# Hybrid decoder step: attention probabilities split to f16 halves by token and turned by DMA instead of TensorE

## The chip, the cores and the metric

The kernel runs on one core of a Trainium2 chip. The metric is the device time of one execution in microseconds (us), and each kernel is quoted with the median of its runs.

## What is computed

Two layers of one mixer each. 2048 prompt tokens (16 tiles of 128) and 32 sample tokens (8 sequences of 4) pass through both.

```python
h = rms_norm(x, norm_g); p = einsum('ntd,de->nte', h, w_in)
qa, ka, va, ga, qb, kb, vb, gb = split(p)
qa = rotary(rms_norm(qa, q_norm_g)); ka = rotary(rms_norm(ka, k_norm_g))
s = where(mask, qa . ka * 64**-0.5, -inf)      # window of 128 tokens, 8 heads on 2 key heads
m = maximum(max(s), sink); e = exp(s - m)
attn = (e / (sum(e) + exp(sink - m))) . va
ret = retention(qb, kb, vb)                    # chunks of 128 tokens, 4 heads
x = x + concat(silu(ga) * attn, silu(gb) * rms_norm(ret)) @ w_out
```

## The kernel before

A layer has four stages, named after the weights in use: A (attention and its gate), B0 and B1 (two retention heads each) and O (the output projection). A stage goes through 17 steps, in A first the sample (step 0), then the 16 prompt tiles. Every engine has its own program written out by hand, and semaphores tie them together.

Numbers of float32 range are carried as two f16 halves, high and low, and a product takes three matmuls. ScalarE writes the high half, VectorE the low one (`scalar_tensor_tensor`: scale, then subtract the high half).

In stage A, while TensorE projects tile s (`proj`, three pieces with 24 matmuls each, in the banks PA and PB by turns), the attention of the tiles before it is put between the pieces:

- `a_T` (L551, L553) transposes q and k of tile s-1 on TensorE. ScalarE's `a_tout` writes their high halves, VectorE's `a_lo` (L943, L945) the low halves.
- `a_S` computes the scores of head group g (0 or 1) in the banks S0 and S1. VectorE's `a_softmax` adds the mask and takes the maximum (L1003), then finds the negative maximum and the sink's share (L1009, L1011). ScalarE's `a_exp` (L1564) makes the probabilities `prob`.
- `a_PT` (L598) turns them by eight f32 transposes on TensorE into X0 and X1. ScalarE's `a_pout` (L1577) and VectorE's `a_plo` (L979) make f16 halves of them, key-wise.
- `a_PV` multiplies by the values into OB. VectorE's `a_mix` has the reciprocal of the sum (L1020 to L1023) and multiplies by the gate (L1043).

VectorE also has, in each step, `a_land_q` (L892, L896), `a_land_k` (L908, L912), a reciprocal square root of 12 small dependent operations (L914, L811 to L817), `a_rotate` (L923 to L937), `a_vcopy` (values to f16, L967 and L968) and `gate` (L957). In eight steps it has `w_low` twice (L851, the next stage's weights), in four others `w_absmax` (L834).

In a helper `Chain`, every small dependent operation is followed at once by a wait for its end. `a_tanh` (L1530) on ScalarE ends a step: it waits for the third piece of the projection, and `gate` waits for it.

In layer 0 the prompt's hidden states are made during stage A: `p_squares` and `p_high` (ScalarE), `p_rstd` and `p_low` (VectorE), `p_T` (L1923, a DMA transpose issued by SyncE). SyncE has one queue, in which these, the loads and the stores of `mix` stand in order. ScalarE's `a_kv` of step 2 waits for the stores of the sample's keys and values (`kvs_out`), which stand behind `p_T(7)` in that queue.

## Time and profile before

| | us |
|---|---|
| median of 3 runs (lowest, highest) | 2010.08 (2008.51, 2020.27) |
| the profiled execution's time | 2014.24 |
| its span, first to last instruction | 2012.4 |
| TensorE busy in the span | 1858.1 (92%) |
| VectorE busy | 1442.5 (72%) |
| ScalarE busy | 712.0 (35%) |

The mean granted TensorE clock is 0.978. Stage A of layer 0 takes roughly 50 to 410 us of the span, that of layer 1 1070 to 1405 us. Busy shares are means over stages whose limits differ: a wait or an engine has to be read inside a stage.

### The profile page before, as it was taken

To read this page: it belongs to the slowest core of one execution; us is meant where nothing else is said; L and a number is where in the kernel's file an instruction comes from. 1 tells how busy PE (TensorE), PEld (TensorE's weight loads), DVE (VectorE), ACT (ScalarE), POOL (GpSimd) and SP (SyncE) were. 2 spreads that over 40 slices of the span, in tenths; PEclk is the share of its full clock that TensorE was granted. 3 is DMA by queue.
4 is the path that set the end of the run, shared out by engine and by line. 5 is a ranking of instruction groups with operands and counts; after the bars stand their busy time and mean duration, and the time that the engine had idled before them with its cause. 6 is when DMAs were issued, how large, how long until landed. Compare 5 with 4: busy or idle time off the path is not lost.

```text
span 2012.4 us, 36841 instructions
## 1 busy us (share of the span) xinstructions
PE 1858.1 (92%) x12264; PEld 1047.5 (52%) x12264; DVE 1442.5 (72%) x4918; ACT 712.0 (35%) x1841; POOL 68.5 (3%) x108
## 2 busy tenths in 40 slices
PE   1778999997999999978998999999999999999999
PEld 0445555553555555543444655555555555555444
DVE  6679899976665666677885899999666657666542
ACT  4444565541232213232442455555213221232110
POOL 3010000010000000021001000001000000000000
PEclk9899999998999999999999999999999999999999
DMA  8332222032000210079994000001210021003864
GB/s 245 67 120 53 58 52 53 16 130 83 11 11 10 98 61 11 11 152 264 242 244 135 8 16 16 10 16 57 78 51 10 10 97 62 11 10 92 225 202 143
DMA packets 203403, 163.03 MB, mean 81 GB/s; under 512 B 145073, under 2 KB 175985, under 8 KB 203153
## 3 DMA queue, kind: packets, MB, share of 16 engines
q1 hardware_dynamic: 193584, 126.33, 23.2%
q0 software_dynamic: 9728, 35.66, 5.4%
q8 instruction: 38, 0.62, 0.1%
q14 instruction: 53, 0.43, 0.1%
HBM read 88.75 MB, written 41.16 MB: 65 GB/s over the span
## 4 chain that ended last, share of the span: by engine, by line
PE 60%; DVE 21%; ACT 4%; issue 4%; DMA 2%; SPq 1%; DVEq 0%; ACTq 0%
PE PA L499 24%; PE PB L499 24%; DVE r L1003 3%; ACT r L1564 2%; DVE r L979 2%; DVE mix L1043 2%; PE S L646 2%; PE OB L665 2%; PE TK L635 1%; PE S L681 1%; PE OB L672 1%; PE X L598 1%; DVE w_mx L834 1%; DMA r<-r 1%; DMA out<-land 1%
## 5 line engine op out<-in xcount | busy, mean ns | idle before, releaser
L499 PE MATMUL PA<-w_a,hT 128*128 128x512 f16 (+1 forms) x1920 | 405.2, 362 | 13.2 <-DVE land L957 13.2
L499 PE MATMUL PB<-w_a,hT 128*128 128x512 f16 (+1 forms) x1920 | 405.2, 362 | 0.0
L499 PEld LDWEIGHTS PA<-w_a,hT 128*128 (+1 forms) x1920 | 186.2, 99 | 187.5 <-DVE land L957 14.1
L499 PEld LDWEIGHTS PB<-w_a,hT 128*128 (+1 forms) x1920 | 185.8, 99 | 180.5 <-issue 11.8
L499 PE MATMUL PA<-w_b,hT 128*128 128x512 f16 x768 | 182.5, 389 | 16.8 <-DVE land L957 16.8
L499 PE MATMUL PA<-w_b,r 128*128 128x512 f16 x768 | 174.4, 384 | 19.4 <-DMA r<-r 17.1
L1564 ACT ACTIVATE r<-r,nm,unqk 128x256 f32<-128x256 f32 x256 | 150.5, 589 | 109.9 <-DVE sd L1011 109.9
L499 PE MATMUL PB<-w_b,hT 128*128 128x512 f16 x768 | 176.3, 379 | 0.0
L1622 ACT ACTIVATE r<-OB 128x128 f32<-128x128 f32 (+1 forms) x136 | 36.3, 272 | 389.8 <-PE S L681 362.4
L499 PE MATMUL PB<-w_b,r 128*128 128x512 f16 x768 | 171.3, 379 | 0.0
L1092 DVE TENSOR_TENSOR r<-S,t_dec 128x256 f32<-128x256 f32 x64 | 27.2, 425 | 154.4 <-PE S L646 154.2
L499 PEld LDWEIGHTS PA<-w_b,r 128*128 128x128 f16 x768 | 75.1, 99 | 114.2 <-DMA r<-r 18.1
L499 PEld LDWEIGHTS PA<-w_b,hT 128*128 (+1 forms) x768 | 76.0, 100 | 106.3 <-DVE land L957 17.2
L499 PEld LDWEIGHTS PB<-w_b,r 128*128 128x128 f16 x768 | 75.0, 98 | 90.1 <-DVE r L1194 0.9
L499 PEld LDWEIGHTS PB<-w_b,hT 128*128 (+1 forms) x768 | 74.8, 98 | 77.2 <-issue 0.4
L1003 DVE CUSTOM_DVE_ANT_0 r<-S,t_ma 128x256 f32<-128x256 f32 x256 | 93.1, 420 | 12.6 <-PE S L586 6.9
L1634 ACT ACTIVATE r<-r,minv 128x1024 f16<-128x1024 f32 (+1 forms) x34 | 39.1, 1149 | 143.0 <-DVE minv L1155 136.4
L1577 ACT ACTIVATE r<-X 128x512 f16<-128x512 f32 x128 | 69.3, 594 | 51.4 <-PE X L598 51.4
L979 DVE SCALAR_TENSOR_TENSOR r<-X,r 128x512 f16<-128x512 f32 x128 | 82.0, 682 | 4.6 <-ACT r L1577 4.6
L586 PE MATMUL S<-kT_hi,r 64*128 64x256 f16 x512 | 54.3, 276 | 27.3 <-DVE r L945 27.3
L598 PE MATMUL X<-eye,r 128*128 128x128 f32 x544 | 71.7, 275 | 7.7 <-ACT es L1567 7.7
L1123 DVE SCALAR_TENSOR_TENSOR r<-r,S 128x128 f32<-128x128 f32 x120 | 29.1, 284 | 60.9 <-PE S L681 60.7
(247 smaller groups left out, 2784.0 us busy)
## 6 DMA issues: line engine op xcount, KB each, us to landing
out<-r SPq DMA_DIRECT2D x40, 512.0 KB, 4.7
r<-mixed SPq DMA_DIRECT2D x32, 512.0 KB, 4.1
r<-in_x_prompt SPq DMA_DIRECT2D x25, 512.0 KB, 4.3
w_b<-in_w_in POOLq DMA_DIRECT2D x16, 512.0 KB, 9.0
mixed<-mix SPq DMA_DIRECT2D x32, 256.0 KB, 2.0
w_a<-in_w_in POOLq DMA_DIRECT2D x16, 512.0 KB, 8.6
mixed<-mix SPq DMA_DIRECT2D x64, 128.0 KB, 1.8
w_b<-in_w_out POOLq DMA_DIRECT2D x16, 512.0 KB, 7.5
```

Of the source, the lines that this page charges most:

```text
L499: last = nc.tensor.matmul(out[0:s.rows, 0:n], lhs, w16(ph, k, p, wpart), start=(k == 0 and part == 0 and wpart == 0), stop=(k == KT - 1 an ...
L586: last = nc.tensor.matmul(SS[kv][:, i * 256:(i + 1) * 256], qT16[d, q, h * P:(h + 1) * P], kT[d, :, :].rearrange("p b t -> p (b t)"), star ...
L598: last = nc.tensor.transpose(XX[q // 4][:, (q % 4) * P:(q % 4 + 1) * P], prob[:, q * P:(q + 1) * P], eye[:, :])
L646: last = nc.tensor.matmul(S0[0:r, h * r:(h + 1) * r], qkT[:, (2 + h) * r:(3 + h) * r], qkT[:, h * r:(h + 1) * r], start=True, stop=True)
L665: nc.tensor.matmul(OB[0:r, h * P:(h + 1) * P], stm[0:r, h * r:(h + 1) * r], v, start=True, stop=s.first)
L979: last = V.scalar_tensor_tensor(out=pT16[:, 1, c], in0=XX[q][:, :], scalar=P_TOP, in1=pT16[:, 0, c], op0=ALU.mult, op1=ALU.subtract)
L1003: last = V.tensor_tensor_reduce(out=prob[:, h * 256:(h + 1) * 256], in0=SS[h // 2][:, (h % 2) * 256:(h % 2) * 256 + 256], in1=m, scale=1.0 ...
L1043: last = V.scalar_tensor_tensor(out=mix[:, b, m:m + A_DIM], in0=OB[:, o:o + A_DIM], scalar=rr[:, g, h:h + 1], in1=land[:, b, A_W + 2 * KV_ ...
L1564: A.activation(x, x, ACT.Exp, scale=unqk[:, 0:1], bias=nm[:, g, h:h + 1], accum_out=rsum[:, g, h:h + 1])
L1577: last = A.activation(pT16[:, 0, c], XX[q][:, :], ACT.Copy, scale=P_TOP)
L1622: last = A.activation(osq[0:r, h * P:(h + 1) * P], OB[0:r, h * P:(h + 1) * P], ACT.Square, accum_out=oss[0:r, h:h + 1])
L1634: A.activation(mh_of(s)[0:r, 0, :], mxt[0:r, b, :], ACT.Copy, scale=minv[0:r, b:b + 1]).then_inc(o_hi, 1)
```

## The change

- The probabilities stay token-wise. ScalarE (`a_phi`) and VectorE (`a_plo`) make the f16 halves from `prob_t` in SBUF, and SyncE issues one DMA transpose for each head group (`prob_T`). `a_PT` and `a_pout` remain for the sample alone. `a_softmax` of a tile waits until the halves of the tile before it, same group, are turned (`a_tp`).
- Scores of group 0 go to S0 and S1, those of group 1 to X0 and X1; `a_PV` of group 1 writes the bank TK. Both scores are issued together, and `a_PV` and `a_mix` of tile s-2 stand in step s.
- VectorE's order in a step is new: `gate` of the tile before comes first, `a_mix` of tile s-2, group 1, last. Waits in chains of small operations are put off, with other work between (`put`, `wait`, `a_norm_link`, `a_rr_link`). The high half of the values moves to ScalarE (`a_vhigh`); `a_rotate` has two wide multiplications in place of four.
- `a_tanh` waits for `a_mix` of tile s-2, both groups, and so does `a_T`.
- In layer 0 the low halves of tiles 4 to 16 move from VectorE to GpSimd (`late_low`, two operations each). The x of tiles 8 to 16 is loaded at the start, in rows of 64 elements, into `hT`. `p_rstd` runs for four groups, not seven. The sinks are loaded before tiles 2 and 3, and the layer's small gain operations (`layer_gains`) stand ahead of the layer.

```diff
 
 RING = 6
...
+CVA = 8
 CVO = 8
 
...
-                        pe.wait_ge(a_po, 2 * an(L, s))
+                        pe.wait_ge(a_po, 2 * L + 2)
                     pe.wait_ge(a_qk, an(L, s) + 1)
                     if not s.first:
-                        pe.wait_ge(a_sm, 2 * an(L, s))
+                        pe.wait_ge(a_sm, 2 * an(L, s) - 1)
+                    if not (s.fixed and s.c < 3):
+                        pe.wait_ge(a_mx, 2 * an(L, s) - 2)
...
+                else:
+                    pe.wait_ge(a_sm, 2 * n)
...
-                                last = nc.tensor.matmul(SS[kv][:, i * 256:(i + 1) * 256],
+                                last = nc.tensor.matmul((SS, XX)[g][kv][:, i * 256:(i + 1) * 256],
...
+                else:
+                    pe.wait_ge(a_tp[g], 16 * tn(L, s) + 16)
+                    if g == 0:
+                        pe.wait_ge(a_vl, tn(L, s) + 1)
+                    pe.wait_ge(a_mx, 2 * n if s.first else 2 * n + g - 1)
...
-            def a_work(L, s, old=True):
-
-
-                late = old and not (s - 2).sample
+            def a_work(L, s):
+
+                t, u = s - 1, s - 2
 
                 def f0():
-                    if old:
-                        a_PV(L, s - 2, 0)
-                    if old and not late:
-                        a_PT(L, s - 2, 1)
-                    if not (s - 1).sample:
-                        a_T(L, s - 1)
-                    if late:
-                        a_PT(L, s - 2, 1)
+                    if not t.sample and u.sample:
+                        a_PV(L, u, 0)
+                        a_PT(L, u, 1)
+                    if not t.sample:
+                        a_T(L, t)
 
                 def f1():
-                    if (s - 1).sample:
-                        a_T(L, s - 1)
+                    if t.sample:
+                        a_T(L, t)
                     else:
-                        a_S(L, s - 1, 0)
+                        a_S(L, t, 0)
+                        a_S(L, t, 1)
 
                 def f2():
-                    if old:
-                        a_PV(L, s - 2, 1)
-                    if (s - 1).sample:
-                        a_S(L, s - 1, 0)
+                    if t.sample:
+                        a_S(L, t, 0)
                         cached_keys(1).then_inc(s_ct, 1)
+                    else:
+                        a_PV(L, u, 1 if u.sample else 0)
 
                 def f3():
-                    a_PT(L, s - 1, 0)
-                    a_S(L, s - 1, 1)
+                    if t.sample:
+                        a_PT(L, t, 0)
+                        a_S(L, t, 1)
+                    elif not u.sample:
+                        a_PV(L, u, 1)
 
                 return [f0, f1, f2, f3]
 
...
+            def a_vlow(L, s):
+
+                v.wait_ge(a_vh, tn(L, s) + 1)
+                V.scalar_tensor_tensor(out=v16[:, s.par, 1, :], in0=land[:, s.par, A_W + KV_W:A_W + 2 * KV_W],
+                                       scalar=cs["A"][:, 2:3], in1=v16[:, s.par, 0, :],
+                                       op0=ALU.mult, op1=ALU.subtract).then_inc(a_vl, 1)
...
-                if s.sample:
-                    return
-                v.wait_ge(a_po, 2 * an(L, s) + g + 1)
-                for q in range(2):
-                    c = slice(q * 512, (q + 1) * 512)
-                    last = V.scalar_tensor_tensor(out=pT16[:, 1, c], in0=XX[q][:, :], scalar=P_TOP,
-                                                  in1=pT16[:, 0, c], op0=ALU.mult, op1=ALU.subtract)
-                last.then_inc(a_pl, 1)
+                v.wait_ge(a_ph, 2 * tn(L, s) + g + 1)
+                V.scalar_tensor_tensor(out=ph16[g][:, 1, :], in0=prob_t[g], scalar=P_TOP, in1=ph16[g][:, 0, :],
+                                       op0=ALU.mult, op1=ALU.subtract).then_inc(a_pl, 1)
...
                 alone(v, a_s, n + 1)
+                if not s.sample and not (s.fixed and L == 0 and s.first):
+                    alone(v, a_tp[g], 16 * tn(L, s))
...
-            for q in range(4):
+            w_absmax(0, "A", 0)
+            w_absmax(0, "A", 1)
+            p_rstd(0)
+            for q in range(2, KT):
                 w_absmax(0, "A", q)
-            p_rstd(0)
+            w_top(0, "A")
             p_low(0)
-            w_absmax(0, "A", 4)
-            w_absmax(0, "A", 5)
-            p_low(1)
-            w_absmax(0, "A", 6)
-            w_absmax(0, "A", 7)
-            w_top(0, "A")
-            p_low(2)
             w_scale(0, "A")
             for q in range(KT):
                 for c in range(3):
                     w_low(0, "A", q, c)
-            p_low(3)
-            v.wait_ge(c_ld, CONST_LOADS * 16)
+                if q in (1, 3, 5):
+                    p_low((q + 1) // 2)
+            v.wait_ge(sk_ld, SINK_LOADS * 16)
+            layer_gains(0)
...
+                def a_first(s):
+
+                    if s.sample:
+                        a_land_q(L, s)
+                        ch = a_land_k(L, s)
+                        gate("A", L, s, 2, A_W, A_W + 2 * KV_W)
+                        a_norm(s, ch)
+                        if L == 0:
+                            v.wait_ge(c_ld, CONST_LOADS * 16)
+                        a_rotate(L, s, ch)
+                        return
+                    a_land_q(L, s)
+                    a_softmax(L, s - 1, 0)
+                    V.memset(v16[:, 0, :, :], 0.0)
+                    ch = a_land_k(L, s)
+                    a_norm(s, ch)
+                    a_rotate(L, s, ch)
+                    a_softmax(L, s - 1, 1)
...
                 def a_step(s, k=None):
-                    if not (s.fixed and s.c < 2):
-                        a_lo(L, s - 1)
-                    a_land_q(L, s)
-                    if not (s.fixed and s.c < 2):
-                        a_plo(L, s - 2, 1)
-                    if not s.sample:
-                        a_softmax(L, s - 1, 0)
-                    if not (s.fixed and s.c < 2):
-                        a_mix(L, s - 2, 1)
-                    if not s.sample:
-                        a_vcopy(L, s - 1)
-                    if k is not None:
-                        w_low(L, "B0", k, 0)
+
+                    t, u = s - 1, s - 2
+                    gate("A", L, t, 2, A_W, A_W + 2 * KV_W)
+                    if u.sample:
+                        a_mix(L, u, 0)
+                        a_lo(L, t)
+                        a_land_q(L, s)
+                        old = a_rr(L, u, 1)
+                        for i in range(3):
+                            a_rr_link(u, 1, old, i)
+                    else:
+                        a_plo(L, u, 1)
+                        m0 = a_rr(L, u, 0)
+                        a_rr_link(u, 0, m0, 0)
+                        a_vlow(L, u)
+                        a_rr_link(u, 0, m0, 1)
+                        a_lo(L, t)
+                        a_rr_link(u, 0, m0, 2)
+                        m1 = a_rr(L, u, 1)
+                        a_rr_link(u, 1, m1, 0)
+                        a_land_q(L, s)
+                        a_rr_link(u, 1, m1, 1)
+                    a_softmax(L, t, 0)
+                    if not u.sample:
+                        a_rr_link(u, 1, m1, 2)
+                    a_softmax(L, t, 1)
                     ch = a_land_k(L, s)
-                    if not s.sample:
-                        a_softmax(L, s - 1, 1)
-                    if not s.sample:
-                        a_plo(L, s - 1, 0)
-                    a_rotate(L, s, ch)
-                    gate("A", L, s, 2, A_W, A_W + 2 * KV_W)
-                    if not s.sample:
-                        a_mix(L, s - 1, 0)
-                    if k is not None:
-                        w_low(L, "B0", k, 1)
-
...
+                    if not u.sample:
+                        a_norm_link(s, ch, 0)
+                        a_mix(L, u, 0, m0)
+                        a_norm_link(s, ch, 1)
+                        if k is not None:
+                            w_low(L, "B0", k, 0)
+                        a_norm_link(s, ch, 2)
+                        if k is not None:
+                            w_low(L, "B0", k, 1)
+                        a_norm_link(s, ch, 3)
+                        a_norm_link(s, ch, 4)
+                        a_norm_link(s, ch, 5)
+                        a_norm_link(s, ch, 6)
...
+                        a_norm_link(s, ch, 11)
+                        a_rotate(L, s, ch)
+                        a_plo(L, t, 0)
+                        a_mix(L, u, 1, m1)
+                    else:
+                        a_norm(s, ch)
+                        a_rotate(L, s, ch)
+                        a_mix(L, u, 1, old)
+                        a_plo(L, t, 0)
...
                 r = s.rows
                 act.wait_ge(pe_piece, piece("A", L, s, 2) + 1)
+                if not (s.fixed and s.c < 2):
+                    act.wait_ge(a_mx, 2 * an(L, s) - 2)
...
+            def a_phi(L, s, g):
+
+                act.wait_ge(a_ex, 2 * an(L, s) + g + 1)
+                A.activation(ph16[g][:, 0, :], prob_t[g], ACT.Copy, scale=P_TOP).then_inc(a_ph, 1)
+
+            def a_vhigh(L, s):
+
+                act.wait_ge(a_pv, 2 * an(L, s))
+                A.activation(v16[:, s.par, 0, :], land[:, s.par, A_W + KV_W:A_W + 2 * KV_W], ACT.Copy,
+                             scale=cs["A"][:, 2:3]).then_inc(a_vh, 1)
...
                 def a_step(s, k=None):
-                    tail, old = not s.sample, not (s.fixed and s.c < 2)
-                    late = old and not (s - 2).sample
-                    if old and not late:
-                        a_pout(L, s - 2, 1)
-                    if tail and not (s - 1).sample:
-                        a_tout(L, s - 1)
-                    if late:
-                        a_pout(L, s - 2, 1)
+
+                    t, u = s - 1, s - 2
+                    if u.sample:
+                        a_pout(L, u, 1)
+                    else:
+                        a_phi(L, u, 1)
+                        a_vhigh(L, u)
+                    a_tout(L, t)
                     a_q(L, s)
-                    if tail and (s - 1).sample:
-                        a_tout(L, s - 1)
                     if k is not None:
                         w_high(L, "B0", k, 0)
                     a_kv(L, s)
-                    if tail:
-                        a_exp(L, s - 1, 0)
-                        if (s - 1).sample:
-                            act.wait_ge(s_ct, L + 1)
-                            cached_keys_out().then_inc(s_ce, 1)
-                        a_pout(L, s - 1, 0)
+                    a_exp(L, t, 0)
+                    a_phi(L, t, 0)
                     if k is not None:
                         w_high(L, "B0", k, 1)
-                    if tail:
-                        a_exp(L, s - 1, 1)
+                    a_exp(L, t, 1)
                     a_tanh(L, s)
 
...
                         p_high(7)
-                    if c in (3, 5, 7, 9, 11):
-                        p_squares(c + 5)
-                        if c < 11:
-                            p_squares(c + 6)
-                    if c in (4, 6, 8, 10, 12):
+                        p_squares(8)
+                        p_squares(9)
+                    if c == 2:
+                        p_squares(10)
+                        p_squares(11)
+                    if c == 3:
+                        p_squares(12)
+                        p_squares(13)
+                    if c == 4:
+                        p_squares(14)
+                        p_squares(15)
+                        p_squares(16)
+                    if 4 <= c <= 12:
                         p_high(c + 4)
...
+            def late_low(n):
+
+                alone(pool, x_hi, n + 1)
+                G.tensor_scalar(x_of(n), x_of(n), py[:, n:n + 1], None, ALU.mult).then_inc(ch_late, 1)
+                alone(pool, ch_late, n - 3)
+                G.tensor_tensor(xh_of(n, 1), x_of(n), xh_of(n, 0), ALU.subtract).then_inc(x_lo, 1)
...
+            def prob_T(L, s, g):
+
+                alone(sp, a_pl, 2 * tn(L, s) + g + 1)
+                alone(sp, a_pv, 2 * an(L, s) if s.first else 2 * an(L, s) + g - 1)
+                sp.dma_start_transpose(pT16[g].rearrange("p e (c t) -> p (e c) t", t=P),
+                                       ph16[g].rearrange("p e n -> p (e n)")).then_inc(a_tp[g], 16)
...
-                for n in range(3, PRO):
+                p_T(3)
+                for n in range(PRO, STEPS):
+                    load_px(n)
+                for n in range(4, PRO):
                     p_T(n)
...
+                def a_step(s):
+                    if not (s.fixed and s.c < 3):
+                        prob_T(L, s - 2, 1)
+                    prob_T(L, s - 1, 0)
+                    if not (s.fixed and s.c < 3):
+                        store_mix("A", L, s - 2)
...
+                    for c in range(2, STEPS):
+                        if 5 <= c <= 13:
+                            p_T(c + 3)
+                        a_step(Step(c))
```

## Rows read from the trace of the kernel before

**Rows 1.** Stretches of both stages A: us; busy PE, PEld, DVE, ACT, POOL; clock; DMA; GB/s
```profile
1190.00:1380.00 190.00, 182.47 (x1611) 112.97 (x1612) 175.49 (x685) 106.94 (x291) 0.35 (x1) 1.00 0.04 14
150.00:395.00 245.00, 220.46 (x1886) 137.50 (x1887) 226.13 (x864) 137.85 (x358) 0.34 (x1) 0.97 0.19 47
```

**Rows 2.** waits in layer 1's attention steps: us in total, times, longest
```profile
DVE r L1003 <- DVE rs L817: 3.4, 14, 0.3
...
DVE r L1003 <- PE S L586: 0.6, 2, 0.4
```

**Rows 3.** timeline of VectorE, one step of layer 1: start us, us
```profile
1345.95 0.75 DVE L892 SCALAR_TENSOR_TENSOR land<-PA,cs_A,qk_g 128x512 f32<-128x512 f32 x1
...
1347.20 1.28 DVE L979 SCALAR_TENSOR_TENSOR r<-X,r 128x512 f16<-128x512 f32 x2
...
1350.23 0.16 DVE L1020 TENSOR_TENSOR rr<-rsum,es 128x4 f32<-128x4 f32 x1
...
1350.90 0.86 DVE L1043 SCALAR_TENSOR_TENSOR mix<-OB,rr,land 128x64 f32<-128x64 f32 x4
1351.67 0.28 DVE L967 TENSOR_SCALAR r<-land,cs_A 128x128 f16<-128x128 f32 x1
1351.98 0.35 DVE L968 SCALAR_TENSOR_TENSOR r<-land,cs_A,r 128x128 f16<-128x128 f32 x1
1352.40 0.75 DVE L851 SCALAR_TENSOR_TENSOR w_b<-w_b,w_gs  x1
1353.07 0.34 DVE L908 SCALAR_TENSOR_TENSOR land<-PB,cs_A,qk_g 128x128 f32<-128x128 f32 x1
...
1353.64 0.17 DVE L914 TENSOR_SCALAR ss<-ss 128x10 f32<-128x10 f32 x1
...
1356.41 0.42 DVE L1003 CUSTOM_DVE_ANT_0 r<-S,t_ma 128x256 f32<-128x256 f32 x1 [0.27 <-DVE rs L817]
...
1365.37 0.75 DVE L892 SCALAR_TENSOR_TENSOR land<-PB,cs_A,qk_g 128x512 f32<-128x512 f32 x1
...
1383.99 0.75 DVE L892 SCALAR_TENSOR_TENSOR land<-PA,cs_A,qk_g 128x512 f32<-128x512 f32 x1 [0.69 <-ACT r L1507]
```

**Rows 4.** timeline of TensorE, the turning of the probabilities in layer 1
```profile
1391.18 1.04 PE L598 MATMUL X<-eye,r 128*128 128x128 f32 x8
```

**Rows 5.** VectorE's L892, once a step: first to last start in a window
```profile
L892 DVE SCALAR_TENSOR_TENSOR land<-PA,cs_A,qk_g x2: 742/742/743, 151.6 to 197.9; 128x512 f32<-128x512 f32 x2
...
L892 DVE SCALAR_TENSOR_TENSOR land<-PA,cs_A,qk_g x2: 740/740/740, 242.7 to 285.9; 128x512 f32<-128x512 f32 x2
...
L892 DVE SCALAR_TENSOR_TENSOR land<-PB,cs_A,qk_g x2: 739/740/740, 307.3 to 349.1; 128x512 f32<-128x512 f32 x2
...
L892 DVE SCALAR_TENSOR_TENSOR land<-PA,cs_A,qk_g x2: 743/747/751, 328.7 to 368.2; 128x512 f32<-128x512 f32 x2
...
L892 DVE SCALAR_TENSOR_TENSOR land<-PA,cs_A,qk_g x2: 745/748/750, 1109.8 to 1150.6; 128x512 f32<-128x512 f32 x2
```

**Rows 6.** timeline of ScalarE: a tanh and the two f16 halves behind it
```profile
87.59 0.67 ACT L1530 ACTIVATE land<-PB,cs_A 128x512 f32<-128x512 f32 x1
88.16 2.17 ACT L1666 ACTIVATE w_b<-w_b,py 128x1024 f16<-128x1024 f32 x2
```

**Rows 7.** timeline of VectorE: a low half, a pair of weight maxima
```profile
50.50 1.28 DVE L1225 SCALAR_TENSOR_TENSOR w_b<-w_b,py 128x1024 f16<-128x1024 f32 x1
...
125.65 2.33 DVE L834 TENSOR_REDUCE w_mx<-w_b 128x1 f32<-128x1024 f32 x2
```

**Rows 8.** issue times and landing of layer 0's DMA transposes, L1923
```profile
L1923 SPq DMA_TRANSPOSE hT<-r x9: 1317/2067/3431, 170.4 to 348.2; - x9
...
DMA to landing us min/median/max: 4.2/4.3/5.4
```

**Rows 9.** ScalarE's wait in step 2 of layer 0
```profile
111.85 0.37 ACT L1522 ACTIVATE r<-PB,cs_A 128x128 f32<-128x128 f32 x1 [13.45 <-DMA out<-land]
```

**Rows 10.** TensorE's wait for the sample step's gate in layer 1
```profile
1078.83 2.74 PE L499 MATMUL PA<-w_a,hT 128*128 128x256 f16 x12 [4.15 <-DVE land L957]
```

553 lines of the change are left out of this document (314 added, 239 removed).

## The prediction

> **What bounds the kernel now.** The change touches only stage A, so I read the busy times by stretches first, in the steady part of each layer's stage A [rows 1]. TensorE is busy 182.5 of 190 us in layer 1 and VectorE 175.5; in layer 0 it is 220.5 and 226.1 of 245. Neither engine can be called the bound from shares so near to each other. Second, the waits of that stretch [rows 2]: VectorE hardly waits for anybody (0.6 us for scores in 290 us; 3.4 us for its own small operations). Third, VectorE's timeline [rows 3]. Its L892 starts once a step. Where it carries two `w_low`, 19.42 us lie between two starts and there is no gap for another engine. In the next step, without them, it is 18.62 us, and VectorE stands 0.69 us at the end: here TensorE sets the time. So TensorE's own step is 18.6 us, VectorE's is 19.4 with and 18.0 without weight work (two `w_low` at 0.67 us, from 1352.40 to 1353.07). In layer 0 the same mark gives 23.2 us a step early on (151.6 to 197.9, two steps), 21.6 in the middle (step 8 at 242.7), 20.9 later (step 13 at 349.1) and 19.1 for step 13 [rows 5], since VectorE also makes the hidden states' low halves, at 1.25 us each [rows 7].
>
> **Part 1, TensorE's transposes go.** Eight take 1.04 us in the list [rows 4], some 0.1 of which lies beside the next matmul; two sets a step are 1.8 us. TensorE's step falls from 18.6 to 16.8 us. Its cover is VectorE: where that is the bound, the gain is nothing.
>
> **Part 2, VectorE's own step.** From 19.42 us I take off: the high half of the values (1351.67 to 1351.98, and a wait), 0.4 us; the three links before each mix, 0.67 us from 1350.23 to 1350.90 and twice a step, of which I expect half to vanish when other work lies between them, 0.7 us; three of the 14 links from 1353.64 to 1356.41 (0.2 us each) put behind large operations, about 0.35 us; and the rotation's two fewer operations, 0.15 us, an estimate at less than one link [rows 3]. `a_plo` now reads SBUF: one operation of 1024 columns at 1.28 us [rows 7] for the present pair at 1.20 (1347.20 to the mask), no gain. That leaves 17.8 us with `w_low`, 16.5 without.
>
> **Part 3, the waits that are added.** This is the term that decides. `a_tanh` of tile s now waits for the mix of tile s-2, group 1, and this mix is the *last* thing in VectorE's step s; `gate` of tile s, which needs the tanh, is the *first* of step s+1. So ScalarE's work between the two lies in the open. I count from the mix's end. The tanh runs from 0.05 to 0.7 us [rows 6], then `gate` may go. The next, `a_plo` of group 1, needs `a_phi`, which stands behind the tanh on ScalarE and is of the size of the L1666 pair's halves, 1.1 us [rows 6]: it ends at 1.8. Without waits `a_plo` would start at 0.5. Cost: 1.3 us a step. Where `w_absmax` (1.15 us each, [rows 7]) or `w_scale` stands between the steps, it fills this hole. A layer 1 step is then 17.8 + 1.3 = 19.1 us with `w_low` (19.4 before), 17.8 without (18.6 before). TensorE at 16.8 us, and `a_T` behind the same mix, stay under this.
>
> Layer 0 has two more. `p_high` stands between tanh and `a_phi` for steps 5 to 13: another 1.1 us [rows 6], so `a_plo` starts at 2.9 and the hole is 2.4 us. And SyncE's queue has `p_T(c+3)` *ahead* of the transpose of the probabilities (u, 1), on whose landing the second `a_softmax` of the same step waits. `p_T` needs GpSimd's two operations, which need that `p_high` (1.8 us). The trace has no such GpSimd operation. VectorE does the work in one operation of 1.28 us; I bound the pair by two of these, 2.5 us, below, and by four, 5.1 us, above, and take 3.8. So the low half is there at 5.6, `p_T` is issued until 7.7 (2.07 us, [rows 8]), and the next transpose lands 4.2 to 5.4 us later [rows 8]: at 12.1 to 13.1, say 12.7. The softmax is reached 6.8 us of work after the mix (gate 0.6, plo 1.2, small ones 0.6, low halves 1.05, q 1.25, first softmax and a link 2.0), plus 2.4: at 9.2. It stands 3.5 us. The step is 16.5 + 1.3 + 2.4 + 3.5 = 23.7 us against 21.3 before. In layer 1 nothing is ahead: (u, 1) is ready at 3.1 us, lands at 7.5, and is wanted at 8.1. Covered, by 0.6 us; if it lands in 5.4 us, that cover is gone.
>
> **Part 4, the openings.** In layer 0, tiles 2 and 3 are loaded behind 18 small loads, which delays the first `p_rstd` and so the weights by 1 to 3 us; earlier gains give that back. ScalarE's wait for the sample's stores lasts until 111.85 us [rows 9]; `p_T(7)` still stands ahead of them, behind GpSimd and nine loads in rows of 64 elements. These cost between the present 4 us and 512 KB in short packets, and I find no net change beyond 2 us, bounds -8 and +10. In layer 1 TensorE stood 4.15 us for the sample's gate [rows 10], which now comes before the norm and the rotation; rotation itself still gates the transposes, so I take 2.7 us.
>
> **The sum.** Layer 1: opening -2.7; steps 2 and 3, 40.8 us before [rows 5] and 35.4 without maxima (17.8 each, less a hole in step 2), -5.4; steps 4 to 6 -0.3 (eight maxima in place of four, 4.6 us more, against 1.5 us a step of part 2 and no hole); step 7 -1.7; steps 8 to 14 seven times -0.3; step 15 +0.5 (it now has `w_low`); the last -0.7. Together -12. Layer 0: up to step 8 -4 (the opening, and `p_low` and four `p_rstd` gone, against three squares that `p_rstd` waits for in step 4); steps 8 to 12 five times 23.7 for the 106.4 us before (242.7 to 349.1, [rows 5]), +12; step 13, with no `p_high` behind it, 22.6 for 19.1, +3.5; the rest 0. Together +12. The stages after A keep their order: their first wait hangs on the store behind the last mix, which moves with it. So 2014.24 us, the profiled execution, becomes 2014; it lies 4.2 us above the median, so against the median, 2009 us.
>
> What a page says of GpSimd: the Trainium skill (GPSIMD Engine Reference, 3.1 Elementwise — side-by-side cycle accounting) gives a `tensor_tensor` of 2048 float32 columns 4497 ns, about 2.25 us for 1024. With a simpler operation of some 1 us ahead of it the pair would take 3.3 us, and the sum would be 4 us lower. No row here shows it.
>
> **The rivals.**
> 1. *The transposes are never late in layer 0* (GpSimd or SyncE faster than my bounds). Then its steps are 20.2 us, and layer 0 gives -16: 1981 us. For it: landing after 4.3 us in the median. Against: the order in SyncE's queue, and 2.07 us of issue.
> 2. *The new waits are hidden too*, VectorE being so late that the tanh is done. It would take 1.3 us from some 24 steps, on top of rival 1: 1950 us. Against: the awaited mix is VectorE's own last operation.
> 3. *GpSimd and VectorE stand in each other's way.* VectorE's `a_plo` at 2.9 us would wait for GpSimd's operation then running, up to 1.9 us (half of 3.8), and the other way round, `p_T` would be later by a 1.2 us `a_plo`. Nine steps by 1.2 us: 2020 us. The trace has no such pair of operations. The Trainium skill (SBUF — State Buffer, Who interferes with whom) says that a VectorE instruction with two SBUF inputs contends with a GpSimd instruction that reads SBUF. `a_plo` had one PSUM input and has two SBUF inputs after the change.
> 4. *Slower: the turning is late everywhere.* GpSimd at 5.1 us and landing at 5.4 make layer 0's step 25.7 us (+2 for nine steps, 18 us); landing over 5 us in layer 1 costs 0.4 to 1 us in 14 steps (10 us); the opening's bound +10 may come on top. 2037 us. It decides from 5.0 us of landing in layer 1 and 13.5 us after the mix in layer 0.
> 5. *The change doesn't do what it says*: TensorE's 1.8 us stay in the chain in another form, since PV is two steps behind but its bank is shared with the transposes. VectorE bounds nearly everywhere, so this is worth under 5 us.
>
> **How the numbers follow.** My forecast, 0.45, holds from 1998 to 2024: GpSimd between its bounds is ±12 us, landing ±5. Rival 1 gets 0.18, rival 2 0.07, rival 3 0.13, rival 4 0.17. The range 1975 to 2037 leaves out rival 2 and the ends of rival 4. A measurement of this kernel can tell about 1% (20 us) from no change. Faster by more: rivals 1 and 2 and a little, 0.28. Slower by more: rival 4 and the ends of 3, 0.22. Within: 0.50.
>
> **What would show it.** In the profile after: no f32 transposes of prompt probabilities; 19.1 us between two marks in layer 1's `w_low` steps, with VectorE idle twice near the gate (for tanh, then for `a_phi`), 1.3 us together; in layer 0 steps of 23 to 24 us, in which the second softmax's first mask waits 3 to 4 us for a DMA; TensorE idle a quarter of that stretch. The prediction is wrong if the mask never waits for a DMA (rival 1), if it also does in layer 1 (rival 4), or if gate follows the mix at once (rival 2).

## The result: 4.8% slower, and the profile after

The changed kernel takes 2108.5 us (median of 4 runs, 2104.1 to 2112.7), the kernel before 2009.3 in the same series: ratio 1.048, 95% interval 1.0447 to 1.0512. The forecast was 2009 us, the range 1975 to 2037. Its profiled execution has a span of 2110.7 us (before 2012.4) and a mean granted clock of 0.947 (0.978).

I first cut both spans at VectorE's first operation of each step (`a_land_q`, L892 before, L930 after), which [rows 5] show for before. All numbers in us:

| | before | after | difference | forecast |
|---|---|---|---|---|
| start to step 0 of layer 0 | 58.7 | 65.1 | +6.4 | in the next row |
| steps 0 to 3 | 92.8 | 95.2 | +2.4 | -4, all up to step 8 |
| steps 4 to 6 | 69.6 | 70.2 | +0.6 | |
| step 7 | 21.6 | 38.5 | +17.0 | |
| steps 8 to 12 | 106.3 | 129.8 | +23.4 | +12 |
| steps 13 to 15 | 56.8 | 63.8 | +7.0 | +3.5 |
| step 16 of layer 0 to step 0 of layer 1 | 666.0 | 683.6 | +17.6 | 0 |
| steps 0 to 7 of layer 1 | 157.6 | 147.4 | -10.2 | -10 |
| steps 8 to 15 | 154.6 | 162.1 | +7.5 | -1.6 |
| step 16 of layer 1 to the end | 628.4 | 655.0 | +26.6 | -0.7 |

Names of the lines after: L1004 `gate`, L1017 `a_plo`, L1051 the mask, L1112 `a_mix`, L889 `w_low`, L872 `w_absmax`, L1646 tanh, L1695 `a_phi`, L1988 and L1990 the two operations of `late_low`, L1983 the all-reduce of the weights' maxima, L486 weights' loads, L2089 `p_T`, L2097 `prob_T`, L2057 `store_mix`, L1788 `p_high`, L1721 ScalarE's first operation on the second piece of a step of stage B (L1598 before), with its tanh (L1725) behind it, for which `gate` waits.

The list of VectorE's waits over the whole span (us in total, times, longest) names the new causes; in [rows 2] it waited for almost nobody in stage A:

```profile
DVE r L1051 <- DMA r<-r: 82.9, 12, 22.4
...
DVE land L1004 <- ACT land L1725: 28.9, 6, 17.4
DVE land L1004 <- ACT land L1646: 19.8, 22, 2.0
DVE w_b L889 <- ACT w_b L1610: 16.8, 16, 1.1
...
DVE r L1017 <- ACT r L1695: 13.3, 21, 2.5
...
DVE pms L1283 <- ACT w_b L1776: 13.8, 1, 13.8
```

The mask's 82.9 us for the turning are 22.4 and 16.3 us at the two ends of stage A, 18.6 in step 7, 21.1 in the six steps after it, and 4.5 elsewhere. The first place to look at is a steady step of layer 0, which answers to [rows 3]. VectorE's timeline (start, length, in brackets the idle time before and who ended it):

```profile
261.04 0.85 DVE L1112 SCALAR_TENSOR_TENSOR mix<-TK,rr,land 128x64 f32<-128x64 f32 x4
...
286.97 0.85 DVE L1112 SCALAR_TENSOR_TENSOR mix<-TK,rr,land 128x64 f32<-128x64 f32 x4
288.64 0.69 DVE L1004 SCALAR_TENSOR_TENSOR land<-land,PA 128x512 f32<-128x512 f32 x1 [0.81 <-ACT land L1646]
290.62 1.42 DVE L1017 SCALAR_TENSOR_TENSOR r<-r 128x1024 f16<-128x1024 f32 x1 [1.29 <-ACT r L1695]
...
293.28 1.75 DVE L1083 TENSOR_SCALAR rr<-rr,cs_A 128x4 f32<-128x4 f32 x1
...
295.01 0.74 DVE L930 SCALAR_TENSOR_TENSOR land<-PB,cs_A,qk_g 128x512 f32<-128x512 f32 x1
...
301.91 0.42 DVE L1051 CUSTOM_DVE_ANT_0 r<-X,t_ma 128x256 f32<-128x256 f32 x1 [3.50 <-DMA r<-r]
...
307.30 0.75 DVE L889 SCALAR_TENSOR_TENSOR w_b<-w_b,w_gs  x1 [1.01 <-ACT w_b L1610]
```

From the mix's end (287.8) `gate` waits 0.81 us for the tanh and `a_plo` 1.29 more for `a_phi`: the hole of the forecast, 2.1 us. The mask of group 1 waits 3.50 for the DMA: also as forecast. But L1083, an operation on 4 columns, takes 1.75 us (0.22 in other steps, as at 233.74), and the second `w_low` waits 1.01 us for ScalarE. GpSimd and SyncE in the same step:

```profile
289.85 2.84 POOL L1988 TENSOR_SCALAR hT<-hT,py 128x1024 f32<-128x1024 f32 x1 [20.78 <-ACT r L1788]
292.88 2.13 POOL L1990 TENSOR_TENSOR r<-hT,r 128x1024 f16<-128x1024 f32 x1 [0.18 <-POOL hT L1988]
```

```profile
295.03 1.78 SPq L2089 DMA_TRANSPOSE hT<-r  x1
```

GpSimd's pair takes 5.16 us (2.84, a gap of 0.18, 2.13), just past the upper bound of the forecast (5.1); L1083 begins in its second operation and ends with it. `p_T` is issued only then, and `prob_T` behind it.

Step 7 is the second place. GpSimd first, then SyncE, then VectorE:

```profile
233.44 0.38 POOL L1983 PARTITION_ALL_REDUCE w_am<-w_m  x1 [26.05 <-issue]
240.52 2.85 POOL L1988 TENSOR_SCALAR hT<-hT,py 128x1024 f32<-128x1024 f32 x1 [6.70 <-issue]
243.55 2.13 POOL L1990 TENSOR_TENSOR r<-hT,r 128x1024 f16<-128x1024 f32 x1 [0.18 <-POOL hT L1988]
```

```profile
245.70 1.32 SPq L2089 DMA_TRANSPOSE hT<-r  x1
```

```profile
227.21 0.16 DVE L883 TENSOR_REDUCE w_m<-w_mx 128x1 f32<-128x8 f32 x1
...
252.60 0.42 DVE L1051 CUSTOM_DVE_ANT_0 r<-X,t_ma 128x256 f32<-128x256 f32 x1 [18.63 <-DMA r<-r]
```

The all-reduce of the B0 weights' maxima has its input at 227.4 and starts at 233.4; the next ordinary operation starts 6.7 us after its end. The low half of tile 10 stands behind both, `p_T` behind the low half, the probabilities behind `p_T`, the mask behind the probabilities: 18.6 us.

The third place is the end of stage A, here in layer 1: GpSimd, SyncE, VectorE, and ScalarE after the change and before it.

```profile
1470.64 5.95 POOL L486 DMA_DIRECT2D w_a<-in_w_in  x8 [196.95 <-DVE land L1004]
```

```profile
1472.03 34.71 SPq L2097 DMA_TRANSPOSE r<-r  x2
...
DMA to landing us min/median/max: 5.1/15.8/26.5
```

```profile
1498.69 0.42 DVE L1051 CUSTOM_DVE_ANT_0 r<-X,t_ma 128x256 f32<-128x256 f32 x1 [22.44 <-DMA r<-r]
```

```profile
1525.91 0.47 ACT L1721 ACTIVATE land<-PA,cs_B 128x256 f32<-128x256 f32 x1 [17.73 <-DMA out<-land]
```

```profile
1430.88 0.47 ACT L1598 ACTIVATE land<-PA,cs_B 128x256 f32<-128x256 f32 x1 [10.69 <-DMA out<-land]
```

GpSimd issues the next weights, eight loads of 512 KB, as soon as the last piece of A has been read, exactly as before the change. But now a transpose of probabilities is issued 1.4 us after the first of them, and lands after 26.5 us; the one issued 2.3 us before the first load landed after 5.1. From VectorE's first operation of step 16 to ScalarE's operation in the last two lines it is 70.2 us, before 46.9; in layer 0 72.3, before 57.5. These two ends of stage A are thus 38 us longer.

The opening is the fourth: VectorE stands 13.8 us for the squares of tile 3 (L1283 above), whose x is now loaded behind the sinks, and step 2 stands for the stores of the sample (ScalarE):

```profile
124.62 0.37 ACT L1636 ACTIVATE r<-PB,cs_A 128x128 f32<-128x128 f32 x1 [13.95 <-DMA out<-land]
```

In [rows 9] this wait ended at 111.85.

### The profile page after: what moved, and what is told of

Read it like the earlier page. It is cut to its first block, busy times and chain, and to the rows that moved or that the text cites. A ratio compares the mean times of both kernels' runs of the same rounds, so it can differ in the third digit from the quotient of the medians.

```text
span 2110.7 us, 36140 instructions
## 1 busy us (share of the span) xinstructions
PE 1837.4 (87%) x11752; PEld 1004.8 (48%) x11752; DVE 1407.4 (67%) x4699; ACT 715.7 (34%) x1809; POOL 134.4 (6%) x134
## 4 chain that ended last, share of the span: by engine, by line
PE 53%; DVE 19%; DMA 8%; issue 6%; ACT 3%; SPq 3%; POOL 2%; DVEq 1%; ACTq 0%; POOLq 0%
PE PB L515 22%; PE PA L515 21%; DMA r<-r 5%; DVE r L1051 3%; DVE mix L1112 2%; PE S L669 1%; PE OB L688 1%; PE TK L658 1%; PE S L704 1%; PE OB L695 1%; DVE r L1017 1%; DVE land L972 1%; POOL hT L1988 1%; DMA hT<-land 1%; DVE w_mx L872 1%
## 5 line engine op out<-in xcount | busy, mean ns | idle before, releaser
L515 PE MATMUL PA<-w_a,hT 128*128 128x512 f16 (+1 forms) x1920 | 416.0, 368 | 18.2 <-DVE land L1004 16.9
L515 PE MATMUL PB<-w_a,hT 128*128 128x512 f16 (+1 forms) x1920 | 422.3, 372 | 8.1 <-DVE land L946 4.6
L515 PEld LDWEIGHTS PB<-w_a,hT 128*128 (+1 forms) x1920 | 190.5, 102 | 200.5 <-issue 30.8
L515 PE MATMUL PB<-w_b,hT 128*128 128x512 f16 x768 | 180.8, 386 | 3.9 <-DVE r L1141 3.9
L1051 DVE CUSTOM_DVE_ANT_0 r<-X,t_ma 128x256 f32<-128x256 f32 x128 | 46.7, 421 | 84.5 <-DMA r<-r 82.9
L1017 DVE SCALAR_TENSOR_TENSOR r<-r 128x1024 f16<-128x1024 f32 x64 | 79.2, 1237 | 13.3 <-ACT r L1695 13.3
L645 PE MATMUL TK<-r 128*128 128x64 f16 x768 | 29.5, 198 | 47.9 <-DMA r<-r 47.9
L541 PE MATMUL PA<-w_a,hT 128*32 128x256 f16 (+1 forms) x336 | 22.0, 343 | 54.1 <-DVE w_a L889 53.3
L1695 ACT ACTIVATE r<-r 128x1024 f16<-128x1024 f32 x64 | 67.3, 1051 | 1.0
```

The source lines that it names most:

```text
L515: last = nc.tensor.matmul(out[0:s.rows, 0:n], lhs, w16(ph, k, p, wpart), start=(k == 0 and part == 0 and wpart == 0), stop=(k == KT - 1 an ...
L541: last = nc.tensor.matmul(quarter(ph, j)[:, 0:CH_A[j][1] if ph == "A" else 256], lhs, w, start=(k == 0 and part == 0 and wpart == 0), stop ...
L645: last = nc.tensor.matmul(OO[g][:, h * A_DIM:(h + 1) * A_DIM], pT16[g][:, e, o:o + P], v16[:, q, ve, h // 2 * A_DIM:(h // 2 + 1) * A_DIM], ...
L1017: V.scalar_tensor_tensor(out=ph16[g][:, 1, :], in0=prob_t[g], scalar=P_TOP, in1=ph16[g][:, 0, :], op0=ALU.mult, op1=ALU.subtract).then_inc ...
L1051: return V.tensor_tensor_reduce(out=prob_t[g][:, h * 256:(h + 1) * 256], in0=(SS, XX)[g][h // 2][:, (h % 2) * 256:(h % 2) * 256 + 256], in ...
L1695: A.activation(ph16[g][:, 0, :], prob_t[g], ACT.Copy, scale=P_TOP).then_inc(a_ph, 1)
```

## The experiments

Each run changes the changed kernel only as its diff says. Ratio is to the kernel before in the same series.

| run | us | ratio (95%) |
|---|---|---|
| the changed kernel | 2108.5 | 1.048 (1.0447 to 1.0512) |
| 1 weights behind the last transposes | 2088.6 | 1.039 (1.0360 to 1.0424) |
| 2 `prob_T` ahead of `p_T` | 2074.5 | 1.034 (1.0298 to 1.0373) |
| 3 low halves of tiles 8 to 16 on VectorE | 2064.7 | 1.026 (1.0213 to 1.0298) |
| 4 last mix first | 2090.8 | 1.040 (1.0353 to 1.0443) |
| 5 weights also behind the last k/v store | 2074.1 | 1.030 (1.0284 to 1.0322) |
| 6 sample's stores first | 2104.6 | 1.045 (1.0431 to 1.0466) |
| 7 tiles 2 and 3 loaded first | 2096.9 | 1.040 (1.0360 to 1.0440) |
| 8 high half early | 2100.2 | 1.044 (1.0413 to 1.0456) |
| 9 all-reduce behind tile 10 | 2099.9 | 1.047 (1.0429 to 1.0508) |
| 10 low halves spread | 2047.9 | 1.020 (1.0160 to 1.0230) |
| 11 all delays out | 1956.1 | 0.974 (0.9710 to 0.9760) |
| 12 the same, GpSimd keeps its low halves | 1966.0 | 0.977 (0.9744 to 0.9801) |
| 13 the same as 12, loop written out | 1958.9 | 0.975 (0.9733 to 0.9771) |
| 14 the changed kernel, loop written out | 2103.3 | 1.046 (1.0424 to 1.0491) |

**Runs 1 and 5: the end of stage A.**

```diff
 pool.wait_ge(dve_piece, free)
+if kind == "B1":
+    for g in range(2):
+        pool.wait_ge(a_tp[g], 16 * (L + 1) * TILES)
+    pool.wait_ge(kv_out, (L + 1) * 32)        # run 5 only
 load_weights(G, kind, nl)
```

> Edit: GpSimd issues the eight 512 KB loads of the B1 weights only when the last transposes of the probabilities of stage A have landed. Theory (transposes stand behind the weights in the DMA engines): in the changed kernel the transpose issued near the first of these loads lands after 20.3 us in layer 0 and 26.5 us in layer 1, the mask of the last tile's group 1 waits 22.4 us in layer 1. Here every transpose at the end of stage A lands after 4 to 6 us, that mask waits under 2 us, and the time falls by 30 to 38 us, to about 2073 us. Rival (the tail is a serial chain of exponentials, low half, transpose and product, whatever else is in flight): landings stay long or the wait only moves, and the time falls by under 8 us. Second rival (the weights are then late for stage B1): the gain at the end of stage A comes back as a wait of the weights' maxima for DMA.

The transposes landed after 4.3 to 6.0 us and the mask's wait was gone (0.4 us at most), but only half of the gain came. ScalarE's wait for the store of the last tile's keys and values, which had been 17.7 us (layer 0: 26.6), grew to 27.8 (35.4), since this store now stood behind the loads (ScalarE's waits of run 1, then of run 5, in layer 1):

```profile
ACT land L1721 <- DMA out<-land: 27.8, 1, 27.8
```

```profile
ACT land L1721 <- DMA out<-land: 17.3, 1, 17.3
```

> Edit: the eight loads of the B1 weights wait for the last transposes of the probabilities and also for the store of the last tile's keys and values. In the first try, with the transposes alone ahead of the weights, the transposes landed after 4.3 to 6.0 us, but ScalarE then waited 35.4 us (layer 0) and 27.8 us (layer 1) for that store, which stood behind the weights in its turn. Theory (short transfers stand behind 4 MB of weights): now both waits are short (store landed within 8 us of its issue), and the time is 30 to 40 us below the changed kernel's 2108 us, about 2073. Rival (the weights are needed by then): the maxima of the B1 weights wait for DMA, and the time stays near the 2089 us of the first try.

From step 16 of layer 1 to the end run 5 takes 629.8 us (before 628.4, after 655.0). In layer 0 the same stretch takes 673.2 (666.0 and 683.6). The weights' maxima do not wait for DMA. One part of the expectation missed: ScalarE's wait is no shorter than in the changed kernel (17.3 for 17.7 us), though the store lands 3.6 us after its issue. What is left of it is time in which the store is not issued yet. The theory holds all the same: from VectorE's first operation of step 16 to the end of that wait it is now 56.4 us in layer 0 and 47.2 in layer 1, as before the change (57.5 and 46.9), so the whole 38 us came from short transfers that were in flight with 4 MB of weights. It is the largest single cause. The two stretches of the first table hold 44 of the 98 us, and two waits give 36 of them back; the rest of layer 0's stretch, where nothing was changed, takes between 604 and 617 us in the runs, so the 7 us that are missing there name no further cause.

**Runs 2 and 3: the order in SyncE's queue, and GpSimd.**

```diff
 def a_step(s, late=None):
     if not (s.fixed and s.c < 3):
         prob_T(L, s - 2, 1)
+    if late is not None:
+        p_T(late)
     prob_T(L, s - 1, 0)
...
-    if 5 <= c <= 13:
-        p_T(c + 3)
-    a_step(Step(c))
+    a_step(Step(c), c + 3 if 5 <= c <= 13 else None)
```

> Edit: in SyncE's queue the transpose of hidden states c+3 goes behind that of the probabilities (u, 1) instead of ahead of it. Theory (order in the queue): the mask of group 1 waits 3.5 us in each of steps 8 to 12 and 18.6 us in step 7 of layer 0, because that transpose stands behind one which waits for GpSimd. Here both waits are gone (under 1 us each), the steps go from 25.9 to 22.4 us, step 7 from 38.6 to about 21, and the time falls by 32 to 38 us, to about 2072 us. Rival (GpSimd's operations and VectorE's in each other's way): the steps stay above 24.5 us and the time falls by under 12 us.

```diff
 gate("A", L, t, 2, A_W, A_W + 2 * KV_W)
...
+    if late is not None:
+        p_low(late)          # steps 5 to 13 of layer 0
     a_plo(L, u, 1)
...
-                    if L == 0 and 4 <= c <= 12:
-                        late_low(c + 4)
```

> Edit: the low halves of hidden states 8 to 16 are made by VectorE in one operation (1.28 us) ahead of the first low half of the probabilities in the next step, not by GpSimd in two (2.84 and 2.13 us); SyncE's order stays. If only the delay counts, the low half is ready 1.3 us and not 5.2 us after the high half, the mask's wait of 3.5 us goes, VectorE's 1.25 us fill the hole in which it waited for ScalarE: steps of 22.4 us. If the two engines also stand in each other's way (one 0.22 us operation of VectorE takes 1.75 us beside GpSimd's second), another 1.7 us goes: 20.7 us a step. Step 7 loses its 18.6 us in both. Time by the first 2070 us, by the second 2057 us. Rival (VectorE is the bound and its work simply adds): steps of 27 us, step 7 alone gains, 2095 us.

Run 2: the mask no longer waits, steps 8 to 12 take 22.6 us each, as the queue theory had it. Step 7 still takes 26.4. There no mask waits for a DMA either. ScalarE's `p_high` of the next tile waits until `p_T(10)` has landed, which is issued only at 243.8, after GpSimd's stall; `a_phi` stands behind it on ScalarE, and VectorE waits 5.05 us for `a_phi` (ScalarE's timeline of run 2):

```profile
248.23 1.15 ACT L1788 ACTIVATE r<-hT,py 128x1024 f16<-128x1024 f32 x1 [5.63 <-DMA hT<-r]
```

Run 3: 21.4 us a step, between its two theories. I had overlooked that this edit also writes out VectorE's steps 8 to 15 of layer 0, which the change had put into a hardware loop; steps 14 and 15, which have no hidden states, fell from 20.2 to 19.1 us with it. Runs 12 to 14 take this apart.

**Run 9: GpSimd's two kinds of work.** `share_max(L, "B0")` of step 6 goes behind `late_low(10)`.

> Edit: in step 6 GpSimd makes the low half of hidden states 10 before the all-reduce of the B0 weights' maxima, not after it. Theory (GpSimd pays 6 to 7 us each time that it changes between this all-reduce and ordinary operations: the all-reduce began 6.1 us after its input was there, the next operation 6.7 us after it, and the low half, which stood behind both, held the transpose in SyncE's queue and VectorE's mask for 18.6 us): here step 7 takes 24 to 26 us instead of 38.6 and the time falls by 12 to 15 us, to about 2095 us; the all-reduce still begins 6 us after GpSimd is free and the next low half about 6.5 us after the all-reduce, but both in the slack of step 7. Rival (the 18.6 us have another cause, as the transposes of that step standing behind other transfers): step 7 stays above 33 us.

Half wrong. Step 7 fell to 20.3 us, but step 8 rose to 34.9, and the time moved by less than its interval. GpSimd's timeline of run 9:

```profile
229.19 2.44 POOL L1990 TENSOR_TENSOR r<-hT,r 128x1024 f16<-128x1024 f32 x1 [0.18 <-POOL hT L1988]
237.55 0.38 POOL L1983 PARTITION_ALL_REDUCE w_am<-w_m  x1 [5.92 <-issue]
257.08 2.85 POOL L1988 TENSOR_SCALAR hT<-hT,py 128x1024 f32<-128x1024 f32 x1 [19.16 <-issue]
```

The all-reduce starts 5.9 us after GpSimd is free, and the low half of tile 11, whose high half ScalarE ended at 249.7, not before 257.1. So the way back is paid when the next ordinary operation comes, not in the idle time before it, and moving the all-reduce moves the stall. A change costs 5.9 to 7.4 us in the four that the rows show (6.1, 6.7, 5.9, 7.4). All traces bear this out: each change leaves records of MODIFY_POOL_CONFIG on GpSimd, and from the first of them to the operation it is 5.6 to 6.0 us toward the all-reduce and 6.7 to 8.2 us back. The kernel before has no ordinary operations on GpSimd but for memsets at its very start, and its all-reduce starts 0.2 us after its input (197.07 and 197.28). The first all-reduce of an execution pays nothing in any run. The Trainium skill (GPSIMD Engine Reference, 2.1 Instruction dispatch) says that the first call of a newly loaded kernel pays about 6 us. The trace agrees toward the all-reduce; the way back is 1 to 2 us dearer than that, and that it comes again at every change is shown by the runs alone.

**Runs 6 and 7: the opening.** Run 6 issues the 16 stores right after `p_T(3)`, ahead of nine loads and `p_T(4)` to `p_T(7)`; run 7 moves `load_px(2)` and `load_px(3)` ahead of the gains and sinks.

> Edit: in layer 0's opening SyncE issues the sample's 16 stores right after its keys are there, ahead of the loads of hidden states 8 to 16 and of the transposes 4 to 7, of which the last waits for GpSimd. Theory (queue order): ScalarE's wait for these stores (13.9 us, until 124.6 us) goes, the mark of step 3 comes at about 128 us and not at 140.8, time about 2096 us. Rival (the transposes 4 to 7 are now later and something else stands: ScalarE for hidden-state transposes, TensorE for tile 4): the mark of step 4 moves by less than 4 us and the time by less than 5.

> Edit: hidden states 2 and 3 are loaded ahead of the gains' and sinks' 20 small loads. Theory: VectorE's first p_rstd waited 13.8 us for ScalarE's squares of tile 3, whose load was issued at 14.4 us and landed at 28; the maxima of the weights stand behind it, so the all-reduce began at 41.3 us and not at 34.2. Here that wait is under 3 us, the all-reduce begins at 34 to 36 us, the first mark comes at 59 us and not at 65, time about 2102 us. Rival (the weights' own loads end then anyway and the two loads only delay them): the all-reduce begins after 39 us, no gain.

Run 7: step 0 starts at 55.2 us, 10 earlier, more than expected. Run 6: ScalarE's wait for the stores is gone, and the mark of step 4 is 1.9 us earlier, no more: the rival. ScalarE now stands 5.9 us for the transpose of tile 4, which is issued behind the nine loads (2.0 us of issue each), and TensorE and VectorE behind ScalarE.

**Runs 4, 8 and 10: the waits at the step's end.** Run 4 exchanges the last two lines of VectorE's step. Run 8 also moves the high half of (t, 1) ahead of the tanh. Run 10 also puts the first low half between the links:

```diff
 # ScalarE, end of a step
     a_exp(L, t, 1)
+    a_phi(L, t, 1)            # runs 8 and 10, was behind the next tanh
     a_tanh(L, s)
 # VectorE
     a_norm_link(s, ch, 2)
-    w_low(L, "B0", k, 1)
+    a_plo(L, t, 0)            # run 10
...
     a_norm_link(s, ch, 8)
+    w_low(L, "B0", k, 1)      # run 10
...
     a_rotate(L, s, ch)
-    a_plo(L, t, 0)
     a_mix(L, u, 1, m1)        # runs 4 and 8: a_plo(L, t, 0) behind it
+    a_plo(L, t, 1)            # runs 8 and 10, was in the next step
```

> Edit: on VectorE the last two operations of a step change places: the mix of tile u, group 1, comes ahead of the low half of tile t, group 0. Theory (the tanh of the next tile waits for this mix, and gate and low half stand behind the tanh): VectorE's waits for the tanh (0.81 us a step, 19.8 us in 22) and for ScalarE's high half (0.26 to 1.29 us a step, 13.3 us in 21) vanish beneath the low half of 1.2 us. Steps with weights go from 20.1 to about 19.0 us in layer 1 and from 25.9 to 24.6 in layer 0; time 2080 us (-20 to -33). Rival (the waits are not on the path, TensorE or a transpose takes them over): steps change by under 0.3 us, time by under 8 us.

> Edit: as the earlier exchange of the last mix and the low half of (t, 0), and besides the high half of (t, 1) on ScalarE goes ahead of the tanh of the next tile and its low half to the end of VectorE's step, so that the transpose of (t, 1) is issued a step's start earlier. In the earlier exchange (2091 us) the hole of 1.0 to 2.1 us a step went, but in layer 1 the mask of group 1 then waited 1.3 us a step for the transpose, 6.3 us after the low half. Theory (the turning takes 6.3 us from the low half, of which the step hid 6.2): now neither waits, layer 1's steps with weights take 18.9 us (the second low half of the weights still waits 1.1 us), layer 0's steps 8 to 12 about 23.5 us (GpSimd's low half is still ahead in SyncE's queue), time 2065 to 2075 us. Rival (TensorE at 16.8 us and a lower clock, or VectorE's own work, is the bound): steps stay at 19.7 us or more, time 2085 us or more.

Run 4's hole vanished as expected, but layer 1's steps only went from 20.4 to 20.0, since the mask of group 1 began to wait for its transpose. Run 8 missed: the mask still waited, and steps took 20.2. VectorE's waits in layer 1, the changed kernel, run 4 and run 8:

```profile
DVE w_b L889 <- ACT w_b L1610: 7.6, 7, 1.1
DVE land L1004 <- ACT land L1646: 5.3, 7, 0.8
...
DVE r L1017 <- ACT r L1695: 1.8, 7, 0.3
```

```profile
DVE r L1051 <- DMA r<-r: 9.3, 7, 1.9
DVE w_b L889 <- ACT w_b L1610: 7.6, 7, 1.1
```

```profile
DVE r L1051 <- DMA r<-r: 7.3, 6, 1.5
DVE w_b L889 <- ACT w_b L1609: 6.5, 6, 1.1
```

In runs 4 and 8 the two low halves are made one behind the other, so the two transposes come to SyncE together. Each holds its queue for 1.9 us, and the second lands 4.3 us later. VectorE's timeline of run 8, the two low halves and the first mask of group 1 behind them:

```profile
1400.41 2.35 DVE L1017 SCALAR_TENSOR_TENSOR r<-r 128x1024 f16<-128x1024 f32 x2
...
1409.62 0.42 DVE L1051 CUSTOM_DVE_ANT_0 r<-X,t_ma 128x256 f32<-128x256 f32 x1 [0.76 <-DMA r<-r]
```

The first low half ends near 1401.6, 8.1 us (twice 1.9, and 4.3) before the mask. Run 10 gives each transpose its own time.

> Edit: as the run with the high half early, but VectorE's low half of (t, 0) goes between the links of the norm, where it waited 1.1 us for ScalarE's second high half of the weights, and that second low half of the weights goes six links later. Theory (in that run and in the exchange before it both low halves came together at the step's end, so that SyncE issued two transposes one after the other at 1.9 us each, and the second landed 8.1 us after the first low half; the mask waited 0.8 to 1.5 us): now each transpose has the queue for itself, lands 6.2 us after its low half and is waited for by nobody, and the weights' wait of 1.1 us is gone. Layer 1's steps with weights take 17.8 to 18.3 us (20.4 in the changed kernel, 19.4 before), layer 1's stage A about 285 us (309.5), time about 2065 us. Rival (TensorE's chain from the last mix by its transposes, ScalarE and VectorE's low halves to the scores has become the bound): steps of 19.3 us or more.

The time is 2048 us, 17 less than expected. Layer 1's steps take 17.7 us, a little under the expected 17.8 to 18.3 (stretches of layer 1's steps with weights: the changed kernel, then run 10):

```profile
1313.00:1455.00 142.00, 127.08 (x1035) 72.40 (x1036) 118.02 (x449) 78.31 (x203) 0.00 (x0) 0.92 0.31 64
```

```profile
1267.00:1410.00 143.00, 134.47 (x1207) 80.37 (x1207) 134.36 (x517) 90.89 (x232) 0.00 (x0) 1.00 0.35 73
```

TensorE and VectorE are both busy 94% now, and the granted clock, 0.92 in the changed kernel's stretch, is back at 1.00. The time is 2.8 points of ratio lower than the changed kernel's, for an edit of some ten lines.

The steps are the smaller part of this. Of the 66 us between the two profiled spans 26 lie in the steps of the two stages A. Another 32 lie at their ends, which take 58.6 and 51.9 us here (72.3 and 70.2 in the changed kernel) and where run 5 took out 38, though this edit leaves the weights' loads alone. The last transpose ahead of the loads is now issued at 1423.79, 0.7 us before the first of them; it lands after 10.6 us, and the mask waits for a quarter of what it did:

```profile
1424.48 5.95 POOL L486 DMA_DIRECT2D w_a<-in_w_in  x8 [177.08 <-DVE land L1004]
...
1434.61 0.43 DVE L1051 CUSTOM_DVE_ANT_0 r<-X,t_ma 128x256 f32<-128x256 f32 x1 [5.68 <-DMA r<-r]
```

So the gains of runs 5 and 10 can't be added.

**Run 11: all of it.** Runs 2, 3, 5, 7 and 10, and the opening anew: the sample's stores behind `p_T(3)`, then the loads of tiles 8 to 11, then `p_T(4)` to `p_T(7)`, whose low halves VectorE makes, then the other loads. GpSimd keeps nothing but loads and all-reduces.

> Edit: all delays that the earlier runs found are taken out at once: B1 weights behind the last transposes and the last store of keys and values, the low halves spread, those of hidden states 4 to 16 on VectorE, their transposes behind that of the probabilities (u, 1), hidden states 2 and 3 loaded first, the sample's stores ahead of hidden states' loads and transposes. If the parts add (end of stage A -36, layer 0's steps -43, opening -10 to -20, layer 1's steps -18, layer 0's steps -15 more), the time is about 1985 us, 1.2% under the kernel before: then the turning by DMA itself was no loss and its price was what it was queued with. Rival (the gain of one part is another's wait, and TensorE's transposes were hidden before): 2009 us or more.

1956 us: 2.65% faster than the kernel before, 29 us below the sum of the expected parts. Its stretches in the order of the first table: 54.7 to step 0, 313.1 in layer 0's stage A (before 347.1), 667.0 between the layers, 289.5 in layer 1's stage A (312.2), 629.5 to the end (628.4). So 57 of the 59 us lie in the two stages A and 4 ahead of them, and the stretches behind them are 2 us longer than before. Steps 13 to 15 of layer 0 take 16.8 us (19.1 or 18.6 before), and there TensorE is the bound, at the 16.8 us that the forecast had for it (windows of run 11):

```profile
334.00:368.00 34.00, 33.68 (x303) 20.03 (x300) 32.97 (x132) 22.72 (x58) 0.00 (x0) 1.00 0.38 79
```

With eight f32 transposes more on TensorE for each group its step was 18.6 us [rows 3]. What VectorE's new order alone would have done to the kernel before, with the transposes left on TensorE, was not tried, so how much of the 2.65% is the turning's own stays open.

**Runs 12 to 14: GpSimd's price and the loop's.**

> Edit: the run with all delays out (1956 us), but the low halves of hidden states 8 to 16 stay on GpSimd as in the changed kernel; 4 to 7 on VectorE. Now nothing of the softmax stands behind them in SyncE's queue. Theory (the two engines stand in each other's way, on top of the order): VectorE is 1.2 us a step cheaper without that work, but 1.7 us dearer for its operations that run beside GpSimd's pair of 5.2 us, so steps 8 to 12 take 18.4 to 18.9 us (18.2 with VectorE's own low half), and step 7 or 8 loses some us more for GpSimd's changes between all-reduce and ordinary operations; time 1960 to 1970 us. Rival (only the order counted, and GpSimd's work is free once nothing stands behind it): steps 8 to 12 take 17.0 us, like steps 13 to 15 (16.8), and the time is 1945 to 1950 us.

> Edit: the run with all delays out and the low halves on GpSimd (1966 us), with VectorE's steps 8 to 15 of layer 0 written out instead of in a hardware loop, as they were before the change and in the run at 1956 us. Theory (loop and contention are two prices: the written-out steps 13 to 15 took 16.8 us, those in a loop 17.6; steps 8 to 12 with GpSimd took 1.1 us more than steps 13 to 15): steps 13 to 15 take 16.8 us, steps 8 to 12 take 17.8 to 18.2, as with VectorE's own low half (18.2), and the time is 1957 to 1960 us. Rival (the 1.1 us were only ScalarE's work or cover in the loop, and GpSimd is free): steps 8 to 12 at 17.2 us or less and a time under 1954.

> Edit: the changed kernel with VectorE's steps 8 to 15 of layer 0 written out, nothing else. Theory (the loop costs VectorE about 1 us a step where VectorE sets the time): steps 14 and 15 go from 20.2 to 19.1 us as in the run with VectorE's low halves, steps 8 to 12, in which the mask waits for SyncE's queue, from 25.9 to about 25, and the time falls by 6 to 9 us, to about 2100. Rival (the 1.1 us in that run came from GpSimd's absence): steps 14 and 15 stay at 20.2.

| steps of layer 0, us | 8 to 12 | 13 to 15 |
|---|---|---|
| run 11: VectorE's low halves, written out | 18.2 | 16.8 |
| run 13: GpSimd's, written out | 18.0 | 16.8 |
| run 12: GpSimd's, in the loop | 18.8 | 17.6 |

(The first of these steps in runs 12 and 13 differs by the all-reduce's stall and is left out: step 8 took 19.8 us in run 12, 20.1 in run 13.) In run 12's step VectorE's L1010 takes 1.14 us beside GpSimd, not 0.34, and L1083 0.70, not 0.22. So GpSimd's low halves cost the step 1.2 us (18.0 less 16.8) and VectorE's own 1.4: of the work that GpSimd takes over nearly all comes back, as slower operations beside it and a short wait for ScalarE. The loop costs VectorE 0.8 us a step where VectorE is the bound. In the changed kernel, where other waits take part of it over, it is 0.5 us in steps 8 to 12 (25.4 for 25.9); step 15 fell to 19.1, step 14 only to 20.0, and run 14's interval overlaps the changed kernel's.

## Why the prediction was wrong

- **The step that failed** is the last sentence of the sum: "The stages after A keep their order: their first wait hangs on the store behind the last mix, which moves with it." The order was kept, but a new kind of work, the last transposes, had come to stand among what is issued at that moment, the weights of B1. The term stood at 0 (-0.7 in layer 1) and measured 17.6 us in layer 0 and 26.6 in layer 1; run 5 gives back 10 and 25 of them, and at the end of stage A itself all of the 38. The prediction took the landing of 4.2 to 5.4 us [rows 8] as a price of the transfer. It is the price in a stretch where the DMA engines are busy for a fifth of the time [rows 1]; among the loads it was 20.3 and 26.5 us. Part 3 asked what stood ahead in SyncE's queue and never what another engine's queue had in flight.
- **Step 7, +17 us.** The prediction counted GpSimd's all-reduce nowhere, although `share_max` stands ahead of `late_low(10)` in the same program. The sum had layer 0 "up to step 8 -4"; it was +26.3 with the opening, and 17.0 of them are this step.
- **The opening, +6.4 us**, was named ("delays the first `p_rstd` and so the weights by 1 to 3 us; earlier gains give that back") and sized at a third. The all-reduce starts at 41.3 us for 34.2 before, and nothing gave it back. That the stores stand behind `p_T(7)` was seen, and judged right: run 6 shows little to be had by their order alone.
- **Layer 0's step** was forecast at 23.7 us and took 25.9. By VectorE's time: its own work 17.6 for 17.8, the hole 2.1 for 2.4, the mask 3.5 for 3.5, and two terms that the sum did not have, the two engines' contention (1.5 us on L1083 and 0.2 on `a_plo`: rival 3, which had 1.2 us a step) and 1.0 us of the second `w_low` for ScalarE. That the mask's wait came out is luck: the step reaches the mask 10.6 us after the mix and not 9.2, and the probabilities are there at 14.1 and not 12.7, since GpSimd's pair took 1.4 us more than assumed. So 1.4 of the 2.2 us came over SyncE's queue; without the contention VectorE would have stood longer for the mask instead (argued from the order of the operations; no run removes it alone). The rule of the Trainium skill in rival 3 (SBUF — State Buffer, Who interferes with whom) fits the slower `a_plo`; L1083 shows that here even an operation on 4 columns is slow.
- **Layer 1's step** was forecast at 19.1 us and took 20.4. VectorE's own work is 17.7 us, forecast 17.8. The hole is 1.0 us, forecast 1.3. But the second `w_low`, which now follows the first with one small link between them, waits 1.1 us for ScalarE's high half, and the mask 0.5 us for the scores. Part 2 moved these operations and did not ask who feeds them.
- **GpSimd** was taken at 3.8 us and measured at 5.16, just past the end of the range (5.1). Its second operation took 2.13 us, near the estimate that the prediction took from the Trainium skill (GPSIMD Engine Reference, 3.1 Elementwise — side-by-side cycle accounting), 2.25; the first was put at some 1 us and took 2.84.
- **Rival 4**, the slower side, had the right sign, "the turning is late everywhere". Its half for layer 0 came true: GpSimd at 5.1 us and a step of 25.7, measured 5.16 and 25.9 (the landing after 5.4 us did not: 4.7 in the step shown above). For layer 1 it had the wrong place: it had later landings in each step of layer 1, where there were none, not one landing of 20 us at each stage's end.
- Part 1 held: in layer 1 TensorE's shorter step was worth nothing as long as VectorE bounded, and its own step is 16.8 us where VectorE lets it.

## What to carry to other kernels

When work moves to DMA, list for each transfer what every engine has in flight at that moment, not only its own queue: a small transfer issued among 4 MB of loads took 20 to 26 us instead of 4.3, and two waits ahead of the loads gave 36 us back. Two transfers that come to a queue together cost the second one the first one's issue (1.9 us here), so their producers belong at different places of the step. The same turning by DMA is 4.8% slower as written and 2.65% faster with its neighbours moved.

## What the runs showed of the hardware

- GpSimd pays each time it changes between an all-reduce over partitions and ordinary operations: 5.6 to 6.0 us from the first record of the change (MODIFY_POOL_CONFIG) to the all-reduce, 6.7 to 8.2 us back to ordinary work, in all 14 traces that have such changes. The way back is paid only when the next operation comes. In the changed kernel it is paid at 76.3 and 233.8 us, in the kernel before and in run 11 never. The first all-reduce of an execution starts 0.13 us after its record.
- A multiplication of 128 x 1024 f32 by a column takes GpSimd 2.84 us, a subtraction with f16 output 2.13.
- A DMA transpose of 128 x 2048 f16 in SBUF holds SyncE's queue for 1.9 us in the median and lands after 4.3 us; 26.5 us when issued among eight loads of 512 KB, 10.6 us when issued 0.7 us ahead of them (run 10).
- A step in VectorE's hardware loop is 0.8 us longer than the same one written out (17.6 and 16.8, runs 12 and 13).
- The mean granted clock fell to 0.92 in layer 1's steps, between the full level and the half one, where TensorE waited 14.6 us in seven steps for the last mix; it was 1.00 before [rows 1] and in run 10 (8.2 us in eight). By the waits the lower clock did not bound these steps: VectorE waited for TensorE only 2.9 us in 142, for scores.
